# Residual and head tiles in rows of 640 columns, wide products cut at a 512-byte line

## The reference

```python
u = rmsnorm(h, g_mix); z = u @ w_in
...
h = h + merged @ w_o
u = rmsnorm(h, g_ffn); hid = causal_dwconv(u @ w_up, ffn_conv_w)
h = h + (silu(hid[..., :D_FF]) * hid[..., D_FF:]) @ w_down
...
h = concatenate([meta, x]); proj = rmsnorm_2(h, norm1_w) @ w_in_2
out_a = hgrn2_mixer(...); out_b = mamba2_mixer(...)
h = h + concatenate([out_a, out_b]) @ w_out_2
h = h + conv_glu_ffn(rmsnorm_2(h, norm2_w), ffn_w_up_2, ...)
y = rmsnorm_2(h, final_norm_w)
```

## Time and profile before

| | us |
|---|---|
| median of three runs | 1782.94 |
| lowest, highest run | 1782.6, 1783.1 |
| profiled execution: span from the first to the last instruction | 1782.0 |
| PE busy in it | 1751.7 (98%) |
| DVE busy | 1172.7 (66%) |
| ACT busy | 717.4 (40%) |

### The profile page before, as it was taken

One profiled execution on the slowest core, in us unless ns is written; L12 is line 12 of the kernel. 1 busy time (PEld: TensorE's weight loads), 2 busy tenths in 40 slices (PEclk: granted clock), 3 DMA queues, 4 the chain that ended last, 5 costly groups with the idle time before them and its releaser, 6 DMA issues.

```text
span 1782.0 us, 27315 instructions
## 1 busy us (share of the span) xinstructions
PE 1751.7 (98%) x11006; PEld 1528.3 (86%) x11006; DVE 1172.7 (66%) x1808; ACT 717.4 (40%) x1100; POOL 11.8 (1%) x12
## 2 busy tenths in 40 slices
PE   8999999999999999999999999999998999999997
PEld 5777777778878888888899999999988999999885
DVE  5666656655567777744476766788797877777332
ACT  6334433332343333333445454544454533333221
POOL 0000000000000000000000000000000000000000
PEclk9999999999999999999999999999999999999999
DMA  6222222223222323333222122222212233223321
GB/s 200 71 79 75 83 83 81 85 83 95 91 87 95 95 95 95 95 106 95 73 85 73 69 63 71 70 72 72 72 64 68 83 95 95 92 88 95 106 95 59
DMA packets 44540, 153.77 MB, mean 86 GB/s; under 512 B 6000, under 2 KB 6384, under 8 KB 44416
## 3 DMA queue, kind: packets, MB, share of 16 engines
q1 hardware_dynamic: 44416, 152.04, 27.4%
HBM read 149.93 MB, written 2.10 MB: 85 GB/s over the span
## 4 chain that ended last, share of the span: by engine, by line
PE 83%; DVE 10%; ACT 3%; DVEq 1%; issue 1%; ACTq 1%; DMA 0%; POOL 0%; SPq 0%
PE ps L647 81%; DVE arena L1358 3%; ACT arena L978 2%; PE ps L651 2%; DVEq L1897 1%; DVE arena L1365 1%; DVE w_lo L1355 1%; ACTq L1338 1%; ACT w_hi L978 1%; DVE h_res L1355 1%; DVE arena L1355 0%; DVE u_lo L1565 0%; ACT L983 0%; DVE arena L1372 0%; DVE r_bc L1355 0%
## 5 line engine op out<-in xcount | busy, mean ns | idle before, releaser
L647 PE MATMUL ps<-u_hi,w_hi 128*128 128x258 f32 (+3 forms) x2376 | 645.6, 325 | 8.2 <-DVE u_lo L1565 6.3
L647 PE MATMUL ps<-u_hi,w_lo 128*128 128x258 f32 (+3 forms) x2376 | 640.4, 323 | 0.0
L647 PE MATMUL ps<-u_lo,w_hi 128*128 128x258 f32 (+3 forms) x2376 | 637.1, 321 | 0.0
L1355 DVE TENSOR_TENSOR w_lo<-w_raw,w_hi 128x1024 fp32r<-128x1024 f32 (+1 forms) x280 | 341.5, 1220 | 153.1 <-ACT w_hi L978 141.3
L647 PEld LDWEIGHTS ps<-u_hi,w_hi 128*128 128x128 f32 (+1 forms) x2376 | 392.8, 188 | 52.7 <-issue 11.9
L647 PEld LDWEIGHTS ps<-u_lo,w_hi 128*128 128x128 f32 (+1 forms) x2376 | 393.8, 188 | 36.7 <-issue 1.1
L647 PEld LDWEIGHTS ps<-u_hi,w_lo 128*128 128x128 f32 (+1 forms) x2376 | 392.6, 187 | 36.6 <-issue 1.6
L978 ACT ACTIVATE w_hi<-w_raw 128x1024 fp32r<-128x1024 f32 (+1 forms) x280 | 293.9, 1050 | 306.7 <-PE ps L647 299.7
L1365 DVE SCALAR_TENSOR_TENSOR ffn<-full,par,ffn 128x512 f32<-128x512 f32 (+2 forms) x176 | 132.3, 751 | 81.5 <-ACT ffn L978 78.3
L978 ACT ACTIVATE arena<-arena 128x528 f32<-128x528 f32 (+11 forms) x189 | 96.2, 531 | 219.5 <-DVE arena L1358 87.1
L978 ACT ACTIVATE ffn<-full,par 128x512 f32<-128x512 f32 x88 | 67.8, 770 | 274.0 <-DVE full L1358 274.0
(11 more groups left out here) (157 smaller groups left out, 1506.0 us busy)
## 6 DMA issues: line engine op xcount, KB each, us to landing
w_raw<-weights SPq DMA_DIRECT2D x279, 512.0 KB, 3.6
h_res<-xT SPq DMA_DIRECT2D x8, 256.0 KB, 4.7
outT<-h_res SPq DMA_DIRECT2D x6, 256.0 KB, 2.4
cst<-consts SPq DMA_DIRECT2D x1, 730.0 KB, 8.7
outT<-ffn SPq DMA_DIRECT2D x2, 256.0 KB, 2.7
seg<-consts SPq DMA_DIRECT2D x1, 256.0 KB, 8.7
par<-params SPq DMA_DIRECT2D x1, 240.0 KB, 6.2
msk<-cmask SPq DMA_DIRECT2D x1, 128.0 KB, 8.9
```

The lines of the kernel that those rows point to most:

```text
L647: return nc.tensor.matmul(out, lhsT, rhs, start=start, stop=stop)
L1355: return V.tensor_tensor(out, a, b, op)
```

## The change

`u_hi`, `u_lo`, `v_hi` and `v_lo` get rows of 640 columns (2560 bytes, five times 512), and each is written and read at shifted columns so that the first column which a product reads lies at the start of a 512-byte line of the tile: in the first block column 16 is put at column 128 of the row, for `norm2` and `v` column 14 at column 0; for `norm1` nothing is shifted. The cut of wide products moves to the next such line: 256 columns in the first half (242 for `hg` and `mz`, which read the `norm1` tile from column 14), and 258 or 272 in the second. The descriptor scratch goes from 16,384 to 1,024 bytes, which makes room for the longer rows; tiles still begin at byte 128 modulo 512.

```diff
-    return first if n <= BANK else first + BANK - halves(n)[0][1]
-def halves(n):
-    half = 2 * -(-n // 4)
-    return [(0, n)] if n <= BANK else [(0, half), (half, n)]
+    return first if n <= BANK else first + BANK - cut_of(g)
+LINE = 128
+def cut_of(g):
+    return 2 * LINE - USED if GROUPS[g][0] in ("hg", "mz") else 2 * LINE
+def halves(n, cut=2 * LINE):
+    return [(0, n)] if n <= BANK else [(0, cut), (cut, n)]
+U_WIDE = 5 * LINE
+U_SHIFT = {"g_mix": LINE - META, "g_ffn": LINE - META, "norm1": 0, "norm2": -USED}
+def u_columns(which, c0, c1):
+    return slice(c0 + U_SHIFT[which], c1 + U_SHIFT[which])
...
-        u_hi = sb("u_hi", [P, KD, T2], F32R)
-        u_lo = sb("u_lo", [P, KD, T2], F32R)
+        u_hi = sb("u_hi", [P, KD, U_WIDE], F32R)
+        u_lo = sb("u_lo", [P, KD, U_WIDE], F32R)
...
-        v_hi = sb("v_hi", [P, KD, T2], F32R, s3)
-        v_lo = sb("v_lo", [P, KD, T2], F32R, s3)
+        v_hi = sb("v_hi", [P, KD, U_WIDE], F32R, s3)[:, :, 0:T2 - USED]
+        v_lo = sb("v_lo", [P, KD, U_WIDE], F32R, s3)[:, :, 0:T2 - USED]
...
-                        hi, lo = u_hi[:, i, c0:c1], u_lo[:, i, c0:c1]
+                        hi, lo = u_hi[:, i, u_columns(which, c0, c1)], u_lo[:, i, u_columns(which, c0, c1)]
...
-                        hi, lo = v_hi[:, i, c0:c1], v_lo[:, i, c0:c1]
+                        hi, lo = v_hi[:, i, c0 - USED:c1 - USED], v_lo[:, i, c0 - USED:c1 - USED]
...
-                    cuts = halves(c1 - c0)
+                    cuts = halves(c1 - c0, cut_of(g))
...
-                f(u_hi[:, k, c0:c1], h_res[:, k, c0:c1], ACT.Identity, scale=gain_of(which, k)).then_inc(u_hi_ok, 1)
+                f(u_hi[:, k, u_columns(which, c0, c1)], h_res[:, k, c0:c1], ACT.Identity, scale=gain_of(which, k)).then_inc(u_hi_ok, 1)
...
-    nc = bacc.Bacc("TRN2", target_bir_lowering=False, num_devices=1)
+    nc = bacc.Bacc("TRN2", target_bir_lowering=False, num_devices=1, dynamic_dma_scratch_size=1024)
```

More of the change, by code:

```diff
@@ L576, in square_parts @@
                 return g_osq, y_hi[:, n, :], y_lo[:, n, :]
-            return h_osq[:, USED:], v_hi[:, n - GLA_H, USED:], v_lo[:, n - GLA_H, USED:]
+            return h_osq[:, USED:], v_hi[:, n - GLA_H, :], v_lo[:, n - GLA_H, :]
         def main(v):
@@ L705, in ga @@
                 for k in range(KD):
-                    hi, lo = u_hi[:, k, META:T2], u_lo[:, k, META:T2]
+                    at = u_columns("g_mix", META, T2)
+                    hi, lo = u_hi[:, k, at], u_lo[:, k, at]
                     cols = slice(GLA_RANK * k, GLA_RANK * (k + 1))
@@ L1320, in ssm_v2 @@
                 act.wait_ge(S["gated"], t + 1)
-                f(v_hi[:, t, USED:], m_y[:, t, USED:], ACT.Identity, scale=pc("m2norm", t)).then_inc(S["v2hi"], 1)
+                f(v_hi[:, t, :], m_y[:, t, USED:], ACT.Identity, scale=pc("m2norm", t)).then_inc(S["v2hi"], 1)
             def ssm_sum(g):
@@ L1564, in raw @@
                 dve.wait_ge(u_hi_ok, KD * i + k + 1)
-                V.scalar_tensor_tensor(out=u_lo[:, k, c0:c1], in0=h_res[:, k, c0:c1], scalar=gain_of(which, k),
-                                       in1=u_hi[:, k, c0:c1], op0=ALU.mult, op1=ALU.subtract).then_inc(u_lo_ok, 1)
+                at = u_columns(which, c0, c1)
+                V.scalar_tensor_tensor(out=u_lo[:, k, at], in0=h_res[:, k, c0:c1], scalar=gain_of(which, k),
+                                       in1=u_hi[:, k, at], op0=ALU.mult, op1=ALU.subtract).then_inc(u_lo_ok, 1)
             def raw_meta(_):
@@ L1770, in head_v @@
                     h_o[:, USED:], h_or[:, USED:], h_gate[:, i % 2, USED:])
-                hi, lo = (y_hi[:, i, :], y_lo[:, i, :]) if gla else (v_hi[:, i, USED:], v_lo[:, i, USED:])
+                hi, lo = (y_hi[:, i, :], y_lo[:, i, :]) if gla else (v_hi[:, i, :], v_lo[:, i, :])
                 link(V.scalar_tensor_tensor(out=o, in0=o, scalar=pc("gla_norm" if gla else "hg_norm", i), in1=r,
@@ L1886, in ssm_v2 @@
                 dve.wait_ge(S["v2hi"], t + 1)
-                V.scalar_tensor_tensor(out=v_lo[:, t, USED:], in0=m_y[:, t, USED:], scalar=pc("m2norm", t), in1=v_hi[:, t, USED:],
+                V.scalar_tensor_tensor(out=v_lo[:, t, :], in0=m_y[:, t, USED:], scalar=pc("m2norm", t), in1=v_hi[:, t, :],
                                        op0=ALU.mult, op1=ALU.subtract).then_inc(tile_lo, 1)
```

## The result

| | before | after |
|---|---|---|
| median of the timed runs, us | 1783.02 | 1775.04 |
| lowest, highest run, us | 1782.6, 1785.88 | 1774.77, 1775.68 |
| ratio, 95% interval | | 0.995 (0.9938 to 0.9962) |
| profiled execution: span, us | 1782.0 | 1772.7 |

A forecast was written before the change was run, and what follows sets the result against it. PE's matmul rate was taken as the bound. 11.1 + 6.2 + 0.4 + 3.2 - 1.5 = 19.4 us less took the span from 1782.0 to 1762.6, the median to 1763.5; forecast's own range 1752 to 1771, 8-in-10 range 1752 to 1778.

The forecast's parts named there:

- Products of 512 columns: First block's 102 products reading `u`: rows fixed at byte 128 approach `a`'s rate, 11.1 us less, between 5.6 and 13.0.
- The other 58 products: 512-column products before the gates and in them: 1392 matmuls, 4 ns less each on average, 5.5 us less.
- In the GLA heads: First-block heads: ACT and DVE work between products, but PE is busy 228.3 of 236 us, so nothing charged.
- Pairs: Wide products in two halves: 258/256 pairs in up2 and `v` 6.2 us less, 264/264 pairs 3.2 us less.
- a rival with a chance of 0.08: Wide products: each half pays the full 13.1 ns, 6.6 us more against 11.1 less, 1778.5 us; chance 0.08.
- the rival that gave only the 512s a gain: Wide products: loading 128 weight columns paces each half whatever its address, so only 11.1 us less, 1772; chance 0.20.
- the 236.7 ns of one unit among seven others: Sign in up2 before: unit beginning 8 bytes before byte 128 modulo 256, 236.7 ns a pair against 238.9 for three before.
- `hg` and `mz`: Their 384 pairs: cut goes to a line, first half stays at byte 184; 1 ns less each, 0.4 us.
- The 1.5 us given back in the state-space stretch: State-space stretch: PE already waits and DVE is at 82%, so half of some 3 us won by pairs is lost.
- The slower rival: All 2712 pairs: a fixed address settles in a bad rhythm, 35.3 us more against 11.1 less, 1807; chance 0.05.
- the rival that nothing changes: `u` against `y`: `u` is slower for another reason than the byte, so the time stays at 1783; chance 0.07.
- Scratch, writers, weights' landing: Smaller scratch, shifted ACT and DVE writes of `u` and `v`, and weights landing in 3.6 us: all costed at nothing.

The follow-up runs named there:

- column 48 with the cut at 264: Changed kernel with pairs of up2, `oh` and `om` moved to column 48 and cut at 264: 1768.14 us, ratio 0.9914 to the kernel before.
- The maps: Two scan runs with output unlike the reference's, giving groups of products different row starts and cuts; 226.7 to 240.0 ns for 512 columns, no kernel time given.
- column 33: Changed kernel with first-block rows fixed at column 33 in place of 128: 1796.72 us, ratio 1.0073 to the kernel before.

## Why the prediction was wrong in size

*Products of 512 columns: right.* Forecast 11.1 us less; the stages show 1.7 + 3.3 + 5.2 = 10.2 less. For up 5.3 ns times 1056 was forecast as 5.6 and is 5.2. The other 58 products were charged at 5.5 and gave 5.0, but by other numbers than I argued: I gave half of them nothing, and all 58 settled, at 226.6 to 228.0 ns against 231.9, more than the 4 ns each that I took; the heads then took 2 us back. That 5.0 lies near 5.5 is luck. "In the GLA heads ... PE is busy there all the same, ... so I charge nothing" was wrong: PE's idle time there grew by 2.1 us.

*Pairs: the step that failed.* "I take the middle of the bounds, 4.3 ns less: 6.2 us" and "the middle, 3.6 less, gives 3.2 us". I let the place that is good for 512 columns be good for halves too. Measured: pairs of 514 in up2 at 240.0 against 238.2, 1.8 ns more, and pairs of 528 at 244.0 against 244.2, no change: in place of 9.4 us less, some 2 us more and nothing. Both are within 2.5 ns of the worst ends of the bounds, 240.4 and 246.2, as if each half paid some 12 to 13 ns over its columns by itself, (240.0 - 214.2) / 2 and (244.0 - 220) / 2, which was a rival with a chance of 0.08. It is no price of a half, though: at column 48 with the cut at 264 two halves cost 233.3. That also answers the rival that gave only the 512s a gain because the weight loads pace a half whatever its address: each half loads 128 weight columns, whether it costs 120.0 ns or 116.7. The middle between two ends was no measurement, and what moved me off the worst end was the 236.7 ns of one unit among seven others. The maps show why such a unit says little: what has a price is a sequence that repeats. Stepping rows repeat one of four units (238.3 ns on average), fixed ones one of their own, at 240.0 here. *`hg` and `mz`* were right: 0.5 to 0.9 ns less against 1 forecast.

*That rival's time was wrong too:* 1778.5 against 1775.04. It charged 2.2 ns to 1824 pairs and 2.9 to 888, 6.6 us. The 1056 of up2 rose by 1.8 ns (1.9 us; the stage shows 1.7), the 384 of `v` cost 0.4 us more, and the others became no dearer. The 1.5 us given back in the state-space stretch fell away with the gain that it was taken from.

*The reason for the first term was incomplete.* "That a constant place is what counts (or that place)": the place counts, and the place is the distance to the weights. That the price before "averages over eight places" was wrong too: modulo 256 bytes there are four, and stepping through them costs more than their mean. The slower rival, a fixed address in a bad rhythm, did not happen in this change, but column 33 is it, 13.3 us slower than before by the medians. The Trainium skill ("TensorE: Matmul & The Clock Gate", Back-to-back issue gap) has N/2.4 + 2.5, 215.8 ns for 512 columns, as the gap of a matmul by itself, and says that in a stream of weight loads and matmuls the spacing is set by both; the rival that nothing changes took the formula alone. Settled, the runs have 226.7 to 240.0 at granted clock 1.00, with a weight load before each matmul. The same page (Step-by-step: what each phase is for) says that the weight load has a read port of its own and takes no read bandwidth from the running matmul; no run here measures the ports, but moving the weights alone by 64 bytes cost `a` 6.7 ns a step, so the place of the weights is not without effect. Why the distance counts, and why modulo 256 bytes, was not shown.

*Scratch, writers, weights' landing: right, nothing.*

## What to carry to other kernels

Where PE is the bound and its row steps are a few per cent over their columns, look at the starts of matmuls for a settled rhythm, and at the distance of the moving row from its weight block modulo 256 bytes: here fixed rows cost from 226.7 to 240.0 ns, and rows that stepped 231.7. Only this kernel's operands (float32r, weight blocks of 128 columns 512 bytes apart) were tried. Don't reason which place is good for another shape or cut; put a scan of places into one run, one place per group, take the cheapest, and time it over a whole stage, since a place can settle at another price there. And price a faster product only where its stage has no other engine just behind it.

## What was unexpected of the hardware

- The step depends on the distance between moving row and weights modulo 256 bytes: 226.7 ns at 0, 240.0 or 236.0 at 132 (column 33), for the same 512 columns. The one shift of both together that was tried, by 64 bytes, changed neither `up` nor the pairs of up2.
- Many settled steps are whole or half multiples of 6.67 ns, 16 columns at 2.4 GHz: 226.7, 230.0, 233.3, 236.7 and 240.0 are 34 to 36 of them, and the pairs' 233.3, 236.7, 240.0, 243.3 and 246.7 are 35 to 37. Others, such as 229.1 or 231.1, are means over a short cycle of unequal steps.
- Cutting 514 columns in 384 and 130 costs 284.5 ns a pair against 240.0 for 256 and 258, though the columns are the same; why was not tried.
- Left open: whether the place in PSUM plays a part (each half's place there moved with the cut), and why the same column settles in two rhythms.
